# Ten row slots of an expert gather ring: five and five, or six for u rows and four for v rows

## The reference, cut to what matters

```python
idx = e1 * N_KEYS + e2                    # 8 heads x 16 picks = 128 experts a token
gates = jax.nn.softmax(top, axis=-1)
def expert_chunk(args):                   # 128 tokens
    xc, ic, gc = args
    u = u_table[ic]                       # rows of 1024 float32
    act = gelu(einsum('cd,chkd->chk', xc, u)) * gc
    v = v_table[ic]
    return einsum('chk,chkd->cd', act, v)
```

## Time and profile before

| | before |
|---|---|
| median of 3 runs | 3488.89 us |
| lowest, highest | 3477.79 us, 3498.98 us |
| the profiled execution | 3507.45 us |
| its span | 3505.6 us |
| mean granted TensorE clock (share of full speed) | 0.834 |
| PE, DVE, ACT, POOL busy | 2507.7, 2067.5, 806.0, 2283.2 us |
| bytes moved, mean rate | 1228.66 MB, 350 GB/s |

### The profile page before, as it was taken

How to read it: one execution, slowest core, us unless ns; L and a number is a source line. 1 busy time by engine, 2 the same in 40 slices (tenths; PEclk the granted TensorE clock), 3 DMA queues, 4 the chain that set the end, 5 groups by cost and what they waited for, 6 DMA issues and landing times.

```text
span 3505.6 us, 32086 instructions
## 1 busy us (share of the span) xinstructions
PE 2507.7 (72%) x10208; PEld 1237.2 (35%) x10208; DVE 2067.5 (59%) x5102; ACT 806.0 (23%) x2575; POOL 2283.2 (65%) x2052
## 2 busy tenths in 40 slices
PE   6896878688786776577665877687666966555555
PEld 5684455244452333233331433233331423111111
DVE  1366457744677556756577656856576647844441
ACT  4323233232333321122111411132112411111111
POOL 0004656776667776777777777777767677777775
PEclk9897999899997889788886987789886988766767
DMA  8355999999999999999999999999999999999998
GB/s 278 113 182 204 366 365 392 346 345 362 373 393 346 364 384 395 379 356 365 377 403 352 363 380 400 366 359 359 398 398 349 329 371 390 351 375 374 368 371 282
DMA packets 390071, 1228.66 MB, mean 350 GB/s; under 512 B 43152, under 2 KB 84112, under 8 KB 389904
## 3 DMA queue, kind: packets, MB, share of 16 engines
q0 software_dynamic: 294912, 1073.87, 81.4%
q1 hardware_dynamic: 90576, 152.34, 12.2%
q10 hardware_dynamic: 4416, 0.40, 0.1%
HBM read 1214.40 MB, written 12.06 MB: 350 GB/s over the span
## 4 chain that ended last, share of the span: by engine, by line
PE 40%; POOL 21%; issue 18%; DMA 13%; DVE 3%; ACT 2%; another core or an unknown queue 1%; ACTq 0%; SPq 0%; DVEq 0%
PE psum L774 19%; POOL big L570 11%; DMA big<-in_peer_v,big 11%; POOL big L559 11%; PE psum L628 6%; PE psum L745 3%; PE psum L667 3%; PE psum L700 3%; PE psum L721 2%; DMA big<-in_w_in 2%; PE psum L684 1%; DVE big L1247 1%; DMA h_scratch<-big 0%; PE psum L594 0%
## 5 line engine op out<-in xcount | busy, mean ns | idle before, releaser
L774 PE MATMUL psum<-big 128*64 128x512 f32 x4096 | 1336.0, 784 | 869.9 <-issue 832.7
L1247 DVE CUSTOM_DVE_ANT_0 big<-big 128x1024 f32<-128x1024 f32 x1024 | 1242.5, 1223 | 735.8 <-DMA big<-in_peer_u,big 692.1
L559 POOL DMA_INDIRECT big<-in_peer_u,big x1024 | 1124.0, 1098 | 709.6 <-issue 299.6
L570 POOL DMA_INDIRECT big<-in_peer_v,big x1024 | 1159.0, 1132 | 502.9 <-issue 266.0
L774 PEld LDWEIGHTS psum<-big 128*64 128x64 f32 x4096 | 335.1, 165 | 1601.8 <-issue 1590.7
L908 ACT ACTIVATE big<-big 128x64 f32<-128x64 f32 x1024 | 297.8, 339 | 1194.7 <-PE psum L774 845.6
L745 PEld LDWEIGHTS psum<-big 128*128 128x128 f32 x2048 | 252.2, 200 | 89.4 <-issue 78.8
L745 PE MATMUL psum<-big 128*128 128x128 f32 x2048 | 270.6, 287 | 10.4 <-ACT big L958 7.8
L628 PE MATMUL psum<-big 128*128 128x256 f32 x960 | 243.1, 406 | 19.9 <-DMA big<-in_w_in 14.7
L1063 DVE CUSTOM_DVE_ANT_0 big<-psum,big 128x128 f32<-128x128 f32 (+7 forms) x128 | 96.9, 757 | 240.2 <-PE psum L667 156.4
L628 PEld LDWEIGHTS psum<-big 128*128 128x128 f32 x960 | 187.0, 202 | 110.6 <-issue 68.2
(11 more groups left out here) (123 smaller groups left out, 1668.7 us busy)
## 6 DMA issues: line engine op xcount, KB each, us to landing
big<-in_w_peer_q SPq DMA_DIRECT2D x128, 512.0 KB
big<-in_w_in SPq DMA_DIRECT2D x24, 1024.0 KB, 5.2
big<-in_peer_u,big POOLq DMA_INDIRECT x1024
big<-in_peer_v,big POOLq DMA_INDIRECT x1024
big<-in_w_out SPq DMA_DIRECT2D x24, 512.0 KB
big<-in_w_in SPq DMA_DIRECT2D x48, 256.0 KB
V<-in_x SPq DMA_DIRECT2D x8, 512.0 KB, 8.2
big<-in_x SPq DMA_DIRECT2D x8, 512.0 KB
```

The source lines that it names most:

```text
L559: nc.gpsimd.indirect_dma_start(out=u_ring[:, g % RU, :], out_offset=None, in_=peer_u, in_offset=bass.IndirectOffsetOnAxis(ap=idx[:, t % 2, ...
L570: nc.gpsimd.indirect_dma_start(out=v_ring[:, g % RV, :], out_offset=None, in_=peer_v, in_offset=bass.IndirectOffsetOnAxis(ap=idx_v[:, t % ...
L774: last = nc.tensor.matmul(pAcc[half_rows(c), n, :], sel[:, (g + c) % RD, :], v_ring[:, (g + c) % RV, n * COLS:(n + 1) * COLS], start=(p == ...
L1247: v.tensor_tensor_reduce(out=row_, in0=row_, in1=hn[:, t % 2, :], scale=1.0, scalar=0.0, op0=ALU.mult, op1=ALU.add, accum_out=dot[:, t % 2 ...
```

## The change

The ten slots are split six and four. Nothing else is edited; every engine keeps its instructions and their order. `u_loaded` and `v_loaded` (one semaphore for each slot) and the two waits `g - RU + 1` and `g - RV + 1` follow from the numbers.

```diff
@@ -37,7 +37,7 @@
 LAG = 24
 LAST_STAGE = TILES + 1
 GROUPS = PICKS // TOPK
-RU = RV = 5
+RU, RV = 6, 4
 RW = 4
 RD = 6
 PAIR = 2
```

## The result

| | before | after |
|---|---|---|
| median | 3483.34 us (4 runs) | 3772.89 us (4 runs) |
| lowest, highest | 3466.28, 3498.98 | 3769.20, 3784.26 |
| profiled execution, span | 3507.45, 3505.6 | 3784.26, 3782.3 |
| PE, DVE, POOL busy | 2507.7, 2067.5, 2283.2 | 2600.9, 2071.2, 2270.1 |
| mean granted clock | 0.834 | 0.803 |

The ratio is **1.0838, with a 95% interval of 1.0779 to 1.0897**: 8.4% slower, where 3.0% was forecast and the range ended at 3740 us. The direction and the place were as forecast, the size was not.

The account below looks back on a forecast made before the run. No single engine bounds the kernel, but the circle of POOL issue, row landing, PE use and slot release; 98 us (long stretch) + 0 (before 1085 us) + 6 (tail) = 104 us, forecast 3593 us against the median, range 3460 to 3740 us.

Parts of the forecast that it names:

- The parity argument: v ring: with four slots the even row waits a whole pair later, for pair k-2; the odd row's condition hardly moves.
- The new circle: Long stretch, end of pair k-2 to end of pair k: four terms, 12.20 us, 6.10 a pair, plus 0.20.
- third term: In the two-pair circle, odd issue's end to the matmul's start: between 3.35 and 5.84 us, taken as 5.4.
- the group of matmuls: Last term of the two-pair circle, PE's eight matmuls for a pair: 2.61 us; single groups 1.94 or 3.68.
- full end: Odd issue's end to matmul on a full memory path: 5.84 us, two pairs in 12.64, 6.32 a pair.
- the mean does not bind: Before 1085 us: 6.78 us a pair lies above the full circle's 6.32, so cost 0, bounds -112 and +42.
- The 0.20 a pair for unevenness: Long stretch: added to 6.10 because circle and pace are equal, about half of the present 0.38, giving 6.30.
- The tail: Kernel's end, v rows only, 4.0 us a pair: 0.62 a pair more over ten pairs, 6 us.
- The attention slots: Where PE is the limit: cover of 1.4 to 3.9 us before PE takes the odd row, so zero cost there.
- Hidden: Rival, chance 0.18: queue thins, issue to use closes at 3.35 to 4.3 us, only the tail's +6 paid, 3495 us.
- Faster by the sixth u slot: Rival, chance 0.10: half of the 112 us of u waits before 1085 us saved, v circle closes, 3439 us.
- Compounding: Rival, chance 0.20: circle at 6.32 plus 0.38 unevenness, 6.70 a pair, 254 us in the long stretch, 3791 us.

## Why the prediction was right or wrong

**The views, the waits and the place: right.** POOL's added waits are for v slots, though after 1085 us they grew by 232 us (413.8 for 181.6) where I had about 100; the u waits shrink without shortening their stretch, and POOL's standing makes DVE wait for u rows. The parity argument is borne out by the run with a gather more between the two v rows: 9% with four slots, 0.3% with five.

**The sum: wrong.** The step that failed is "The new circle", in its third term, the time from the odd issue's end to the matmuls. The stretch before 1085 us, put at 0, and the group of matmuls were mis-sized too.

1. *From the odd issue's end to the matmuls.* I took 5.4 us, "under the full end, because a slower pace thins the queue". In the changed trace the mean is 5.96 us. Of these the landing takes 5.63, up to the last rise of the semaphore that PE waits for. The trace before lacks many of these rises, but both traces have the record of every packet that the queue moved: the last one of an odd row ends 4.95 us after the issue in the changed trace and 5.03 us in the one before. The rate fell by 8% and this time by 0.1 us: there was next to no thinning. Why a row takes so long with others in flight, no run shows apart. That my upper end, 5.84, comes so near is luck. It was a misreading: the group at 1729.61 has no idle time of PE before it, PE came to it late from other matmuls, and the packets of its odd row had ended at 1727.78, 4.0 us after the issue.
2. *The group of matmuls.* I took 2.61 us from the mean of the whole program before. In the long stretch the mean is 2.78, and it was 2.71 there before. So 0.10 us is the wrong stretch for the mean. The other 0.07 goes with the clock: a group takes 1.94 us at a granted clock of 1.0 and 3.68 at 0.5, PE's idle time before the groups rose from 869.9 to 1079.4 us, and the granted clock of the stretch is 0.79 where it was 0.80. That is a small compounding that I had only in the rival.
3. *Before 1085 us: "the mean does not bind", 0.* It did bind: 209 v rows in the time of 221, (1085 - 335) / 104.5 = 7.18 us a pair for 6.78, some 42 us. That was my upper bound. I had set the 6.32 of the long stretch against 6.78. In this stretch the four parts are 0.58 + 3.90 + 7.52 + 2.43 = 14.43, 7.2 a pair, with 6.5 us to the landing alone: the circle itself is longer here.

The other two terms of the circle held: the issues measured 3.96 for 3.95. The 0.20 a pair for unevenness, a guess from half of 0.38, is in the trace the mean of 0.61 us, and not 0.24, from the group's end to the even issue, 0.19 a pair. From the forecast's 6.30 to the 6.65 measured, the flight adds 0.28 and the group 0.08. By the windows the long stretch costs (6.65 - 6.05) x 391 = 235 us. But the two windows do not hold the same rows, and the later rows go faster in both kernels. Followed row by row, the changed kernel is 41 us late at v row 221 and 261 us at row 1003: the long stretch costs **220 us**, not 98.

4. *The tail.* Forecast 6 us. POOL now stands 5.5 us once in four rows:

```profile
3733.77 0.94 POOL L570 DMA_INDIRECT big<-in_peer_v,big  x1 [5.29 <-PE psum L774]
...
3744.30 0.93 POOL L570 DMA_INDIRECT big<-in_peer_v,big  x1 [5.50 <-PE psum L774]
```
```profile
3740.39 6.36 PE L774 MATMUL psum<-big 128*64 128x512 f32 x16 [4.01 <-issue]
```

10.53 us for two pairs, 5.27 a pair against 4.0: 13 us for ten pairs, and followed by the same rows it is 13.0 too. The circle's terms are 0.24, 2.17 for the two issues, 4.45 (3735.94 to 3740.39, not the 3.35 of the lone last row) and 3.68 for the first of the two groups in this line, 10.54 in all. The second group belongs to the other circle. Here the clock counts for much: the granted clock from 3717 to 3769 us is 0.67, where it was 0.85 in the same rows before (3456 to 3495 us), and a group takes 3.23 us on average over the last ten pairs, where it took 2.29.

**Together**, by rows, 42 us up to v row 221, 220 to row 1003 and 13 to the last row, less 1.2 us at the first v row and with 2.6 us after the last: the spans differ by 276.7 us.

**The attention slots.** The cover worked out there was not tested by itself.

**The rivals.** "Hidden" fell: from the issue's end to the use it takes 5.96 us, where closing under POOL's pace wanted about 4.3. "Faster by the sixth u slot" fell: it is worth nothing beside four v slots (3769.05 and 3769.04 us) and 0.1% beside five (3534.97 and 3530.90), both within the intervals. "Compounding" came near with 3791 us, and had half the right cause: the circle does stay at its full end, and the clock adds to it; but the late u rows that I gave as its first reason cause nothing. Part of the agreement is luck: it put 254 us on the long stretch, which costs 220, and its full end of 6.32 rests on the misread row.

**The pages.** The 358 GB/s of the Trainium skill (DMA: Bandwidth & Descriptors, "Where 436 GB/s comes from") is not a ceiling here: before, 371 GB/s were held for 2365 us on the one core at work, and the change, at 340, was slower. What it is with other cores at work no run here shows. The estimate of 3.2 us worked out from the fixed and variable cost in the Trainium skill (DMA: Bandwidth & Descriptors, "Anatomy of one DMA") is near the 3.35 us of the lone last row; with neighbours in flight the landing took 5.63 us on average.

## What to carry to other kernels

Count ring slots in the units in which they are given back: four rows used two by two are two slots, and the odd fifth row was half a unit of lead, worth 7 to 8%; the sixth row on the other side was worth nothing. Write down the circle (release, issues in program order up to the last row needed, flight, use) and divide it by the units in the ring; if it is above the present pace, expect it as the new pace, here 13.31 us over two units. Take the flight as a mean under load, in the same stretch, from rows where the user stood waiting for it: a use that came late because the user was busy does not measure it. What an in-order issuing engine does between the first and the last row of a unit is part of that circle, and moving it out gave back two thirds of the loss (164 of 246 us) without any memory.

## What the runs showed of the hardware that I had not expected

- The flight of a 512 KB gather hardly changed between 371 and 340 GB/s: from the issue's end to the last packet the odd v rows took 5.03 us before and 4.95 us in the change. It is not a constant of the chip, though: the lone last row took 3.35 us up to its use, and the odd rows took 5.8 us to the last packet in the kernel with three weight slots, five u and six v slots, at 373 GB/s.
- The changed kernel's median moved by 0.1% between two occasions (3772.89 and 3769.04 us), that of the kernel before by 1.3% over five (3483 to 3530 us). That the circle holds the one steady is a guess.
- POOL's issues take 0.94 us at the median and now and then up to 2.7 us, 1.10 to 1.13 us on average, in both kernels. In a circle they count with their mean.
- With the matmuls of a pair written row by row, both counts still came with the last two matmuls, 0.06 us apart, at the group's end.
